# Expert stage of an encoder layer: gate-up rounds by token group and ff quarter, gated rows and tokens turned by VectorE

## The reference

```python
def expert_choice_ffn(h, w_router, w_gate, w_up, w_down):
    ...
    cap = CAPACITY_FACTOR * n_tok // N_EXPERTS        # 64 and 32 tokens of the two groups
    aff, idx = lax.top_k(probs.T, cap)
    xe = t[idx]
    hid = jax.nn.silu(jnp.einsum("ecd,edf->ecf", xe, w_gate)) * jnp.einsum("ecd,edf->ecf", xe, w_up)
    ye = jnp.einsum("ecf,efd->ecd", hid, w_down) * aff[..., None].astype(h.dtype)
    out = jnp.zeros_like(t).at[idx.reshape(-1)].add(ye.reshape(-1, d))
```

## Time and profile before

| what | value |
|---|---|
| median of three runs | 2559.37 us |
| the profiled execution | 2561.34 us |
| its span | 2559.5 us |
| mean granted TensorE clock | 0.993 |
| PE busy | 2516.5 us (98%) |
| DVE, ACT, POOL busy | 977.0, 618.0, 303.1 us |
| moved by DMA | 708.09 MB, of it 628.92 MB on SP's queue (q1) |

### The profile page before, as it was taken

How to read it: one execution, slowest core, us unless ns; L and a number is a source line. 1 busy time by engine, 2 the same in 40 slices (tenths; PEclk the granted TensorE clock), 3 DMA queues, 4 the chain that set the end, 5 groups by cost and what they waited for, 6 DMA issues and landing times. The chain is left out here.

```text
span 2559.5 us, 66707 instructions
## 1 busy us (share of the span) xinstructions
PE 2516.5 (98%) x30079; PEld 1815.0 (71%) x30079; DVE 977.0 (38%) x1944; ACT 618.0 (24%) x1458; POOL 303.1 (12%) x419
## 2 busy tenths in 40 slices
PE   9899999999999999899999999999999999999997
PEld 9788899889988888566656666566566666565664
DVE  6989888988887343301111111111110111011012
ACT  5345444544445121111111111111111111111111
POOL 0322332233321000000000000000000000000001
PEclk9899999999999999999999999999999999999998
DMA  4233223323447443899999999999999999999993
GB/s 176 62 111 124 89 98 112 124 88 99 135 140 260 136 152 117 339 413 410 421 417 397 404 372 386 382 384 387 381 383 382 380 390 379 380 388 382 377 386 124
DMA packets 72428, 708.09 MB, mean 277 GB/s; under 512 B 9840, under 2 KB 14064, under 8 KB 49616
## 3 DMA queue, kind: packets, MB, share of 16 engines
q1 hardware_dynamic: 49232, 628.92, 61.6%
q0 software_dynamic: 14272, 56.60, 7.2%
q10 hardware_dynamic: 8640, 18.29, 1.9%
HBM read 669.72 MB, written 34.06 MB: 275 GB/s over the span
## 5 line engine op out<-in xcount | busy, mean ns | idle before, releaser
L2378 PE MATMUL p_gu<-more,xT 128*32 128x256 f32 x9600 | 627.0, 381 | 0.0
L2303 DVE SCALAR_TENSOR_TENSOR tg<-tg,p_gu 128x128 f32<-128x128 f32 x264 | 76.1, 288 | 1288.6 <-ACT tg L2252 1288.6
L2378 PE MATMUL p_gu<-raw,xT 128*32 128x256 f32 x7296 | 489.7, 382 | 0.9 <-DVE xT L2342 0.9
L2378 PEld LDWEIGHTS p_gu<-more,xT 128*32 128x32 f32 x9600 | 337.4, 110 | 180.5
L2378 PEld LDWEIGHTS p_gu<-raw,xT 128*32 128x32 f32 x7296 | 262.8, 110 | 138.5 <-issue 2.3
L1090 PE MATMUL pp<-h_hi,wx_hi 128*128 128x256 f32 (+1 forms) x832 | 295.7, 355 | 0.5 <-ACT fo L676 0.5
L2401 PE MATMUL p_y<-more,hidT 128*32 128x384 f32 x2400 | 284.7, 486 | 0.0
L1090 PE MATMUL pp<-h_hi,wx_lo 128*128 128x256 f32 (+1 forms) x832 | 282.6, 340 | 0.0
L1090 PE MATMUL pp<-h_lo,wx_hi 128*128 128x256 f32 (+1 forms) x832 | 281.6, 338 | 0.0
L2259 ACT ACTIVATE hidT<-p_h 128x128 f32<-128x128 f32 x264 | 73.3, 278 | 862.1 <-PE p_h L2388 858.2
L2401 PE MATMUL p_y<-raw,hidT 128*32 128x384 f32 x1824 | 216.2, 486 | 0.0
(11 more groups left out here) (285 smaller groups left out, 3764.0 us busy)
## 6 DMA issues: line engine op xcount, KB each, us to landing
more<-in_w_e SPq DMA_DIRECT2D x100, 3072.0 KB, 12.8
raw<-in_w_e SPq DMA_DIRECT2D x76, 3072.0 KB
w_raw<-in_w_x SPq DMA_DIRECT2D x48, 512.0 KB, 3.6
dec<-acs POOLq DMA_DIRECT2D x48, 512.0 KB, 4.9
w_raw<-in_w_g SPq DMA_DIRECT2D x24, 512.0 KB, 3.5
g_tab<-gx POOLq DMA_DIRECT2D x8, 1152.0 KB, 6.0
w_raw<-in_w_s SPq DMA_DIRECT2D x16, 512.0 KB, 3.8
gx<-fo ACTq DMA_DIRECT2D x16, 384.0 KB, 2.8
```

What stands on the lines that cost most here:

```text
L2303: dve.scalar_tensor_tensor(out=tg[:, r % 2, :], in0=tg[:, r % 2, :], scalar=1.0, in1=p_gu[r % 2][:, 0:P], op0=ALU.add, op1=ALU.mult).then_ ...
L2378: mm = pe.matmul(p_gu[r % 2][quad(q), 0:2 * P], xT[:, t // FT % 2, k * SLOTS + 32 * g:k * SLOTS + 32 * (g + 1)], weights(t)[:, k * 2 * P:( ...
```

## The change

A round now is one token group g for one block b of four ff tiles (or three: the 22 tiles of an expert are blocks of 4, 4, 4, 4, 3, 3). All four strips hold the same 32 tokens; strip q streams quarter q (32 columns) of each tile of the block, gate and up, that is 256 columns, or 192 in the blocks of three. There are 288 rounds, 18 for each expert. With this placement turning each 32 x 32 square of the gated rows gives ff on the partitions, and DVE does that in one transpose a round; TensorE's turns, ACT's copies and the PSUM between them are gone. The tokens of the next expert are turned by DVE too, in twelve transposes spread over three rounds in the middle of an expert. A block's weights come in three loads (gate and up for k = 0 to 3, the same for k = 4 to 7, down) of 2 MB (16 KB a row) or 1.5 MB (12 KB a row), into ten slots of 16 KB. The gate-up slots come free when the block's rounds are done, the down slot after its down products. TensorE's order is: round (b, 0), all down products of block b-1, rounds (b, 1) and (b, 2). At the end ACT squares, and DVE norms, two tiles a round over three rounds, and the x loads wait for the gate-up of the third last block.

```diff
-UT = 2
-NU = FT // UT
+BLOCKS = (4, 4, 4, 4, 3, 3)
+NB = len(BLOCKS)
+PARTS = 3 * NB * E
 EARLY_RAW = 3
-RAW = 7
-TW = P * (2 * KD + KD)
-UW = UT * TW
+HELD_RAW = 4
+RAW = 10
+CW = max(BLOCKS) * D
 QUADS = 4
 GROUPS = SLOTS // 32
-JOBS = GROUPS * FT * E
-ROUNDS = JOBS // QUADS
-HELD = 4
...
-def load_unit(sp, A, raw, s_raw, e, u):
-    slot = (NU * e + u) % RAW
-    src = A["w_e"][e:e + 1, u * UW * P:(u + 1) * UW * P].rearrange("e (p n) -> p (e n)", p=P)
-    sp.dma_start(raw[slot], src).then_inc(s_raw[slot], 16)
+def load_part(sp, A, raw, s_raw, c):
+    b, part = divmod(c, 3)
+    e, i = divmod(b, NB)
+    w = BLOCKS[i] * D
+    at = (3 * sum(BLOCKS[:i]) * D + part * w) * P
+    src = A["w_e"][e:e + 1, at:at + w * P].rearrange("e (p n) -> p (e n)", p=P)
+    sp.dma_start(raw[c % RAW][:, 0:w], src).then_inc(s_raw[c % RAW], 16)
...
-        more = a.sb("more", [P, RAW - EARLY_RAW, UW])
-        raw = [*raw, more[:, 2], more[:, 3], more[:, 0], more[:, 1]]
+        more = a.sb("more", [P, RAW - HELD_RAW, CW])
+        raw = [*raw, *(more[:, i] for i in (3, 4, 5, 0, 1, 2))]
+        a.sb("between", [P, 2048])
...
+        places = [raw[(PARTS - 10 + i) % RAW][:, j * D:(j + 1) * D] for i in range(3) for j in range(4)]
+        xf, of = places[0:NT], places[NT:2 * NT]
...
+        def wide(r):
+            return 32 * BLOCKS[r // GROUPS % NB]
+        def tiles_to(b):
+            return FT * (b // NB) + sum(BLOCKS[:b % NB])
...
+            def load(c):
+                b, part = divmod(c - RAW, 3)
+                sp.wait_ge(*((s_gu, GROUPS * (b + 1)) if part < 2 else (s_dn, tiles_to(b + 1))))
+                load_part(sp, A, raw, s_raw, c)
+            load_part(sp, A, raw, s_raw, 3)
             listed(sp)
-            load_unit(sp, A, raw, s_raw, 0, 3)
-            load_unit(sp, A, raw, s_raw, 0, 4)
+            for c in range(4, 7):
+                load_part(sp, A, raw, s_raw, c)
             sp.wait_ge(s_xt, 1)
...
+            for c in range(RAW, PARTS):
+                load(c)
+            sp.wait_ge(s_gu, ROUNDS - 2 * GROUPS)
+            sp.wait_ge(s_dn, tiles_to(NB * E - 3))
...
+                w = wide(r)
+                act.activation(tg[:, r % 2, 0:w], p_gu[r % 2][:, 0:w], ACT.Tanh, scale=0.5).then_inc(s_tg, 1)
...
+                if 0 <= r - SQUARES_AT < 3:
+                    square(2 * (r - SQUARES_AT))
+                    square(2 * (r - SQUARES_AT) + 1)
...
+                w, p = wide(r), p_gu[r % 2]
                 dve.wait_ge(s_tg, r + 1)
-                dve.scalar_tensor_tensor(out=tg[:, r % 2, :], in0=tg[:, r % 2, :], scalar=1.0, in1=p_gu[r % 2][:, 0:P],
+                dve.scalar_tensor_tensor(out=tg[:, r % 2, 0:w], in0=tg[:, r % 2, 0:w], scalar=1.0, in1=p[:, 0:w],
                                          op0=ALU.add, op1=ALU.mult).then_inc(s_sg, 1)
                 dve.wait_ge(s_sg, r + 1)
                 if r >= 2:
-                    dve.wait_ge(s_t, r - 1)
-                dve.scalar_tensor_tensor(out=hid[:, r % 2, :], in0=tg[:, r % 2, :], scalar=0.5,
-                                         in1=p_gu[r % 2][:, P:2 * P], op0=ALU.mult, op1=ALU.mult).then_inc(s_hid, 1)
+                    dve.wait_ge(s_hT, r - 1)
+                dve.scalar_tensor_tensor(out=hid[:, r % 2, 0:w], in0=tg[:, r % 2, 0:w], scalar=0.5,
+                                         in1=p[:, w:2 * w], op0=ALU.mult, op1=ALU.mult).then_inc(s_hid, 1)
+                dve.wait_ge(s_hid, r + 1)
+                if r >= 2 * GROUPS:
+                    dve.wait_ge(s_dn, tiles_to(r // GROUPS - 1))
+                dve.transpose(hT[:, r % (2 * GROUPS), 0:w], hid[:, r % 2, 0:w]).then_inc(s_hT, 1)
+            def tokens(e, g):
+                if g == 0:
+                    dve.wait_ge(s_g, 16 * e + 32)
+                    dve.wait_ge(s_gu, GROUPS * NB * (e - 1))
+                for q in range(QUADS):
+                    ins = dve.transpose(tiles(xT[quad(q), e % 2, :])[:, :, quad(g)],
+                                        xe[quad(g), 0:D].rearrange("p (k q s) -> p k q s", q=QUADS, s=32)[:, :, q, :])
+                if g == GROUPS - 1:
+                    ins.then_inc(s_xt, 1)
...
-                if r >= NORMS_AT:
-                    norm(r - NORMS_AT)
-            norm(NT - 1)
+                for e in range(1, E):
+                    if 0 <= r - tokens_at(e) < GROUPS:
+                        tokens(e, r - tokens_at(e))
+                if 0 <= r - NORMS_AT < 3:
+                    norm(2 * (r - NORMS_AT))
+                    norm(2 * (r - NORMS_AT) + 1)
...
-            def turn(r):
-                pe.wait_ge(s_hid, r + 1)
-                if r >= 1:
-                    pe.wait_ge(s_hT, r)
-                pe.transpose(p_h[:, 0:P], hid[:, r % 2, :], ident[:]).then_inc(s_t, 1)
...
+            def gate_up(b, g):
+                r, e, w = GROUPS * b + g, b // NB, 2 * wide(GROUPS * b)
+                if r >= 2:
+                    pe.wait_ge(s_hid, r - 1)
+                if g == 0 and b % NB == 0:
+                    pe.wait_ge(*((s_xt, e + 2) if e else (s_xc, 2)))
+                for k in range(KD):
+                    if g == 0 and k % (KD // 2) == 0:
+                        loaded(b, k // (KD // 2))
+                    for q in range(QUADS):
+                        at = (k % (KD // 2) * QUADS + q) * w
+                        mm = pe.matmul(p_gu[r % 2][quad(q), 0:w], xT[:, e % 2, k * SLOTS + 32 * g:k * SLOTS + 32 * (g + 1)],
+                                       part(b, k // (KD // 2))[:, at:at + w], start=(k == 0), stop=(k == KD - 1))
+                mm.then_inc(s_gu, 1)
...
+            def down(b, tiles):
+                if b and b % NB == 0:
+                    pe.wait_ge(s_ye, 2 * (b // NB))
+                loaded(b, 2)
+                pe.wait_ge(s_hT, GROUPS * (b + 1))
+                for i in tiles:
+                    added(b, i, 0)
+                    added(b, i, 1).then_inc(s_dn, 1)
...
+            for b in range(NB * E):
+                gate_up(b, 0)
+                if b and b < NB * E - 1:
+                    down(b - 1, range(BLOCKS[(b - 1) % NB]))
+                gate_up(b, 1)
+                gate_up(b, 2)
+            b = NB * E - 1
+            down(b - 1, range(BLOCKS[(b - 1) % NB]))
+            down(b, range(BLOCKS[b % NB] - 1))
+            for half in range(2):
+                added(b, BLOCKS[b % NB] - 1, half).then_inc(f_y, 1)
...
+        raw_t = a.sb("raw", [P, HELD_RAW, CW])
+        raw = [raw_t[:, i] for i in range(HELD_RAW)]
...
+    gu = np.stack([gate, up], axis=4).reshape(E, KD, P, FT, 2, QUADS, 32).transpose(0, 2, 1, 5, 4, 3, 6)
+    parts, t0 = [], 0
+    for n in BLOCKS:
+        own = gu[..., t0:t0 + n, :].reshape(E, P, 2, -1)
+        parts += [own[:, :, 0].reshape(E, -1), own[:, :, 1].reshape(E, -1),
+                  down[:, t0:t0 + n].transpose(0, 2, 1, 3).reshape(E, -1)]
+        t0 += n
+    w_e = np.concatenate(parts, axis=1)
```

More of the change, by code:

```diff
@@ L2172, in _ @@
                 sp.wait_ge(f_o, t + 1)
[L2173 removed]
+                sp.dma_start(out[0, row:row + P, :], of[t]).then_inc(f_out, 16)
             sp.wait_ge(f_out, 16 * NT)
@@ L2383, in turn, with part @@
-            def turn(r):
-                pe.wait_ge(s_hid, r + 1)
-                if r >= 1:
-                    pe.wait_ge(s_hT, r)
-                pe.transpose(p_h[:, 0:P], hid[:, r % 2, :], ident[:]).then_inc(s_t, 1)
-            def hidden(t, g):
-                r, q = divmod(job(t, g), QUADS)
-                return hT[:, r % HELD, quad(q)]
-            def added(t, b):
-                f = t % FT
-                w = weights(t)[:, 2 * KD * P:TW]
-                pe.wait_ge(s_hT, turned_by(t) + 1)
+            def part(b, i):
+                return raw[(3 * b + i) % RAW]
@@ new lines, in loaded @@
+            def loaded(b, i):
+                c = 3 * b + i
+                pe.wait_ge(s_raw[c % RAW], 16 * (c // RAW + 1))
+            def gate_up(b, g):
[12 more added lines that the diff above has]
+                mm.then_inc(s_gu, 1)
@@ L2400, in added, with hidden @@
+            def added(b, i, half):
+                first, last = (b % NB == 0 and i == 0), (b % NB == NB - 1 and i == BLOCKS[b % NB] - 1)
+                w = part(b, 2)[:, i * D:(i + 1) * D]
+                def hidden(g):
+                    return hT[:, (GROUPS * b + g) % (2 * GROUPS), quad(i)]
                 for g in range(GROUPS):
-                    pe.matmul(y_first[b][quad(g), :], hidden(t, g), w[:, b * 3 * P:(b + 1) * 3 * P],
-                              start=(f == 0), stop=(f == FT - 1))
@@ L2403, in added @@
-                for g in ((0, 1), (2,))[b]:
-                    mm = pe.matmul(y_last[g], hidden(t, g), w[:, LAST_AT:D], start=(f == 0), stop=(f == FT - 1))
-                return mm
-            def down(t):
-                if t and t % FT == 0:
-                    pe.wait_ge(s_ye, 2 * (t // FT))
-                added(t, 0)
-                added(t, 1).then_inc(s_dn, 1)
```

(45 more changed lines are left out.)

86 lines of the change are left out of this document (17 added, 69 removed).

## The result

The changed kernel takes 2480.82 us (median of 4 runs, 2479.53 to 2483.16) against 2559.86 us in the same session (4 runs). The ratio is 0.9691, interval 0.9674 to 0.9708. The gain is 79 us where 95 were forecast; the time lies in the range, 17 us above the forecast. The profiled execution took 2479.53 us with a span of 2477.6.

A forecast was written before the change was run, and what follows sets the result against it. TensorE was the bound; relieved to 85.1 us an expert, it yields to the weight stream at 86.5. Stream start 1042.3 + 16 x 86.5 + 1.3 gives 2427.6; the end brings 2464 us, range 2442 to 2512.

The forecast's parts named there:

- What goes from TensorE: Turns (6.9 us an expert) and token transposes (about 1.0) leave TensorE, which then needs 85.1 us in place of 92.96.
- The work on DVE and ACT: DVE's new transposes, 0.29 us a round plus token turns, stay hidden and ACT loses work: cost 0.
- rival (c): Gate-up rounds of three tiles cost as much as those of four: 90.3 us of TensorE an expert, 2517 us; chance 0.08.
- (d): Gate-up rounds: strips overlap only while sharing weight columns, so slower, about 3340 us; chance 0.06 with the load rule.
- That the bound changes hands: In the expert stage the weight stream, 86.5 us an expert, becomes the bound over TensorE's 85.1.
- Rival (a): TensorE stays the bound, SP's queue being faster than read (over 407 GB/s): 2434 us; chance 0.07.
- Rival (e): Nothing comes of it: the weight stream was the true bound all along, at 384 GB/s; 2559 us; chance 0.03.
- The price of a load: Weight loads get smaller and more numerous: 0.05 us fixed for each, +0.4 us an expert.
- rival (b): Smaller weight loads cost 0.46 us each: 89.3 us an expert, end at 2509 us; chance 0.12.
- The stream's pace: SP's queue moves weights at 401.9 GB/s, so 34.60 MB an expert take 86.1 us before the added load cost.
- How the waits look: From about the eighth expert on TensorE waits in each block for the second gate-up load, some 0.3 us.
- The end: Late x holds ACT's squares ahead of gating, costing some 8 us; last matmuls 2446.6, plus 17.1 us tail, span 2463.7.

The follow-up runs named there:

- cut: The changed kernel, but from the 31st load on only three quarters of each load's columns are fetched: 2452.3 us, ratio 0.9576.
- quiet: The changed kernel without GpSimd's gathers of experts 2 to 15 and scatters of experts 0 to 14: 2445.22 us, ratio 0.9553.
- split: The changed kernel with every weight load issued as two of half the columns: 2493.24 us, ratio 0.9738.
- mid: The changed kernel with squares and norms two rounds later, two of the norms after the last round: 2476.89 us, ratio 0.9677.

## Why the prediction came out as it did

**What goes from TensorE: right.** 85.1 us was the sum, 85.53 is its own pace in cut and quiet; 7.4 us an expert went, forecast 7.9 (6.9 and 1.0). (The 213 ns that the prediction takes for a strip's record stand in none of its rows; its own 1.68 ns a column gives 215, and the step holds with it.) That the turn's price is lost overlap, 0.42 us a round and not the 0.33 of its record, is what the earlier trace rows said; rounds now take 3.45 us.

**The work on DVE and ACT: right, at nothing.** The round's transpose took 0.31 us for the 0.29 taken, the tokens' 432 ns; TensorE waits for neither in the stage. Rounds of 192 columns ran in proportion (2.60), so rival (c) is out; four different streams overlap in full (3.45), so (d) is out.

**That the bound changes hands: right.** Rival (a), TensorE stays the bound, needed 407 GB/s. That pace exists, in the faster half of the engines (406.6), and does no good. Rival (e) is out by 5.6 us an expert.

**The price of a load: right.** 0.05 us by split; rival (b) is out, and so are the 2.0 us for each load that the prediction worked out beside it.

**The stream's pace: the term that was mis-sized.** "SP's queue moved 72.35 MB in 180 us, 401.9 GB/s by the wall. An expert is 34.60 MB: 86.1 us." The reading was right and its use wrong: it is the mean of two halves that drift apart, and the consumer waits for the slower. In the trace of before that half had 398.9 GB/s in the full queue, which is 86.7 us; with 0.4 for the smaller loads 87.1, and measured are 87.4. Of the 0.9 us that were missing in an expert, 0.6 come from mean against slower half. Of the other 0.3 an estimate from the instruction packets gives most: an expert took 12.1 of them, where at the rate of before, 0.125 a us, 86.7 us have 10.8; 1.3 more at some 1.55 us on eight engines are 0.25 us. The relieved TensorE works through its program faster, and its instructions are fetched over the engines that were already behind. 16 x 0.9 = 14.4 us is the 13.8 by which the last weights came later than forecast. The trace of before had the lag: 7.9 us between the first and the last landing of a load at 1320 us, of which bytes over time say nothing.

**How the waits look: half right.** In place of some 0.3 us in each block, 21 waits of the weight loads in 1000 us, 1.0 us in the mean and 2.4 at most; their sum, 21.9 us, is what 0.3 in each of some 69 blocks would be.

**The end: right in sum, by luck.** The mechanism is there: x seen and squared late, the gating of round 284 behind it, TensorE waiting twice. So is the sum, 36.2 us for 36.1. The squares' share is 4.2 us (mid), not 8: without them the last matmuls would have come 15.6 us after the last weights and not 10.4. The stretch without the squares was taken too short by about as much as the squares were taken too long, and the one error hid the other.

## What to carry over

When a transfer stream is about to become the bound, its pace is that of the slowest part of a load: look at the spread of one load's landings in a full queue, not at bytes over time. And count what else rides on the same engines, the program's own instructions among it: more and shorter matmuls cost the weight stream too. Before taking work off the bounding engine, work out the runner-up's pace; here TensorE was relieved of 7.4 x 16 = 118 us and the kernel gained 79; of the 39 between, cut gives back 28.5, so these went to the stream; the other 10 were not taken apart. A step that waits for the last transfer must not stand ahead of work that the bound needs, but moved to the very end it can become the end itself.

## What the runs showed of the hardware

Half of the sixteen DMA engines were 2.6% slower with the weights than the others whenever the queue had no pauses (395.9 against 406.6 GB/s), with and without GpSimd's transfers, and the distance grew until the slots were full. The Trainium skill (DMA: Bandwidth & Descriptors, Latency and other measured facts) names two engines, 7 and 15, as usually slower, and guesses at GpSimd's descriptors; the landings here show eight, and quiet shows it without nearly all of GpSimd's transfers. The eight are those behind whose weight packets the instruction packets stand (102 of 102 that can be told apart, in four traces), one packet of 16 KB for 256 TensorE instructions; the numbers of these engines the records don't tell. GpSimd's row transfers, 0.8 MB an expert, cost the stream 4.2 us. DVE turns 128 x 128 float32 in 32 x 32 blocks in 0.31 us, hardly more than the 0.29 it takes for a gated product of that size.
